# State-space scan at half the tokens, tiles in pairs, in the first layer of a three-block network

## Chip, cores, metric

One core of one Trainium2 chip. The metric is the device time of one execution in microseconds. Everything is fp32. The change touches one stage, the first mixing layer (class Fox in the code), which takes about the first 190 us of the kernel.

## The reference, cut to what matters

The network runs three blocks over 256 tokens of width 1024. The first block's mixer joins an attention with a forget gate (8 heads of 64) and a diagonal complex state-space scan over 32 groups of 16 channels with 64 states each:

```python
def s5_scan(u, a_re, a_im, log_dt, b_re, b_im, c_re, c_im, d_skip):
    dt = jnp.exp(log_dt)[:, None]
    mag = jnp.exp(a_re * dt)
    lb_re = mag * jnp.cos(a_im * dt)
    lb_im = mag * jnp.sin(a_im * dt)
    ...
    bu_re = jnp.einsum('bsgc,gpc->bsgp', u, bb_re)
    bu_im = jnp.einsum('bsgc,gpc->bsgp', u, bb_im)
    ...
    _, _, h_re, h_im = lax.associative_scan(combine, (a_re_t, a_im_t, bu_re, bu_im), axis=1)
    y = jnp.einsum('bsgp,gcp->bsgc', h_re, c_re) - jnp.einsum('bsgp,gcp->bsgc', h_im, c_im)
    return y + d_skip * u

def fox_s5_mixer(x, w_in, f_bias, ...):
    z = x @ w_in
    q, k, v, f_logit, u = jnp.split(z, ...)
    att = forgetting_attention(q, k, v, f_logit + f_bias)
    y = jax.nn.gelu(s5_scan(u, ...))
    y = y * jax.nn.sigmoid(y @ w_glu + b_glu)
    return jnp.concatenate([att, y], axis=-1) @ w_out
```

That is h(t) = L h(t-1) + B u(t), y(t) = Re(C h(t)), with a complex L per state.

## The kernel before, in words

All phases are written out by hand, one instruction stream per engine, with semaphores between them. Weights come through a ring of twelve 1 MB slots, filled by SyncE's DMA queue (L3019); a slot is filled again when the product that read it has ended. In this layer four slots are lent out as scratch memory, so eight are in use.

The scan works in tiles: 16 tiles j, each two groups (128 states on the partitions), with k = j // 4 and m = j % 4. A tile's two groups have 32 channels, which lie on partitions 32m to 32m+31 of `uT`. Instead of a complex recurrence the kernel turns the input by a phase table (cosine and sine of the angle of L times the token's place), scans with the real magnitude alone, and turns back:

- `tile_input` (L796): PE, two products of 32 rows by 256 tokens, real and imaginary part, into a bank.
- `turn_in` (L1143): VectorE, three operations on 512, 256 and 256 columns (L1155 to L1157).
- POOL adds the two halves (L1171), 512 columns.
- `scan` (L1161): VectorE, two scans over 256 tokens (L1166).
- `turn_back` (L1183): POOL, two products of 512 columns (L1193, L1194).
- `tile_output` (L805): PE, four products with 32 output columns each, side by side in the four 32-column groups of the array (L812 to L815); below, four such products are a quad.
- `keep_turn` (L828): ScalarE copies the four strips with signs.
- `tile_sums` (L818): PE, after every fourth tile, four products with a folding matrix, again side by side (L824).
- `y_keep` (L1135): VectorE, adds the skip term.

The order around it: `tensor` (L839) computes u (`first_product`, L925), the small strips for the forget gate (L281), tile inputs 0 and 1, the q and k projections (L268), then v in halves (L301) with tiles between them. Then comes the loop over tiles 3 to 15. Eight of its steps also carry an attention head: `scores` (L578: L588 and L790), `turn_p` (L593: L598) and `head_out` (L601: L606 and L608); on VectorE `head_max` (L624) and `head_scale` (L645), on ScalarE `head_exps`, `head_weigh`, `head_turned`, `head_kept` (L684 to L719). After the loop `mix_part` (L942: L946) starts the output product, then the gate (`fox_glu`) and the rest.

VectorE first prepares, from L1030 on: magnitude, sine and cosine, the output matrix times (L - 1)/a (`Cz`, 128x512), and the phase table for tokens 128 to 255 by seven doublings (`while n < P`, L1077). ScalarE mirrors it to the lower half (`mirror`, L1006). `Steps` (L67) makes each instruction of VectorE, ScalarE and POOL wait for the one before it on its engine.

Banks 0 and 1 hold the tile inputs, bank 2 sums, bank 3 outputs, banks 4 to 7 all else, each pair or set taken in turn.

Of the kernel before, what the change touches and what calls it, by code (L numbers as in the profile page):

```python
# [12 lines left out]
ACT = mybir.ActivationFunctionType  # L13
# [4 lines left out]
P = 128  # L18
SEQ = 256
# [329 lines left out]
class Start(Phase):  # L349
# [36 lines left out]
    def sync_second(self, sp):  # L386

        net, io, fox = self.net, self.net.io, self.net.phase_objects[1]
        for n, dst in enumerate(fox.C):
            sp.dma_start(dst, io["s5_c"][n].rearrange("p (k n) -> p k n", k=16)).then_inc(fox.s("params_loaded"), 16)  # L390
# [335 lines left out]
class Fox(Residual, Heads):  # L726
# [5 lines left out]
    HEAD_BEHIND = {5: 0, 6: 1, 8: 2, 9: 3, 10: 4, 12: 5, 13: 6, 14: 7}  # L732
# [4 lines left out]
    def __init__(self, net):  # L737
# [3 lines left out]
        self.uT = a.take(4 * SEQ, 4, SEQ)  # L741
# [4 lines left out]
        self.Cz = [a.take(512, 16, 32) for _ in range(2)]  # L746
        self.ut = a.take(1024)
        self.g = [self.ut[:, 0:512], self.ut[:, 512:1024], a.take(512)]
        self.t = a.take(512)
        self.w = a.take(20 * 16, 20, 16)  # L750
        self.ph = [a.take(16 * SEQ, 16, SEQ) for _ in range(2)]

        b = Arena(net.ring, self.LENT * UNIT)
        odd = [b.take(512) for _ in range(2)]
        self.C = [h.rearrange("p (a b) -> p a b", a=16) for h in odd]
        self.alloc_heads(b)
        self.sel = b.take(8 * P, 8, P, rows=8)
        self.ft = [b.take(SEQ, rows=8) for _ in range(6)]
        self.c_rows = b.take(16, NT, 8)
        self.strips = [b.take(SEQ) for _ in range(3)] + [a.take(SEQ)]  # L760
        self.f_strips = self.strips[0]
        self.turned = [[b.take(512) for _ in range(2)], odd]
        self.yT = self.catT[:, 4:8, :]
        self.mask = net.causal[:, :]
        self.sig = [self.B[0].rearrange("p a b -> p (a b)"), self.B[1].rearrange("p a b -> p (a b)")]

# [29 lines left out]
    def tile_input(self, pe, j):  # L796

        k, m = divmod(j, 4)
        t = self.net.T.open(pe, ("bu", j), self.INPUT)
# [3 lines left out]
        self.net.T.close(("bu", j), mm)  # L803

    def tile_output(self, pe, j):  # L805

        T = self.net.T
        t = T.open(pe, ("turn", j), self.TURN)
        pe.wait_ge(self.s("h_ready"), j + 1)
        by_cos, by_sin = self.turned[j % 2]  # L810
        re, im = slice(0, SEQ), slice(SEQ, 2 * SEQ)
        pe.matmul(t[0:32, re], self.Cz[0][:, j, :], by_cos[:, re], start=True, stop=True, skip_group_check=True)  # L812
        pe.matmul(t[32:64, re], self.Cz[1][:, j, :], by_cos[:, im], start=True, stop=True, skip_group_check=True)
        pe.matmul(t[64:96, re], self.Cz[1][:, j, :], by_sin[:, re], start=True, stop=True, skip_group_check=True)
        T.close(("turn", j), pe.matmul(t[96:128, re], self.Cz[0][:, j, :], by_sin[:, im], start=True, stop=True,  # L815
                                       skip_group_check=True))

    def tile_sums(self, pe, k):  # L818

        T = self.net.T  # L820
        t = T.open(pe, ("y", k), self.SUMS)
        pe.wait_ge(self.s("turn_kept"), 4 * k + 4)
        for m in range(4):
            mm = pe.matmul(t[32 * m:32 * m + 32, 0:SEQ], self.net.fold[:, 0:32], self.strips[m], start=True, stop=True,  # L824
                           skip_group_check=True)
        T.close(("y", k), mm)

    def keep_turn(self, act, j):  # L828

        net, T = self.net, self.net.T  # L830
        k, m = divmod(j, 4)
        if k:
            T.take(act, ("y", k - 1))
        t = T.take(act, ("turn", j))
        net.ac(act.activation(self.strips[m], t[:, 0:SEQ], ACT.Copy, scale=self.w[:, 19, 0:1]))
        T.free(act, ("turn", j))
        act.sem_inc(self.s("turn_kept"), 1)

    def tensor(self, pe):  # L839
# [5 lines left out]
        pe.wait_ge(self.s("params_loaded"), 16 * 4)  # L845
        pe.wait_ge(self.s("u_kept"), 4)
        for j in range(2):
            self.tile_input(pe, j)
# [4 lines left out]
        self.tile_input(pe, 2)  # L853
        vs = [net.use_unit(pe) for _ in range(2)]
        t = T.open(pe, ("fox_v", 0), rest)
        net.part(pe, t, vs, net.xT, 0, range(4))
        self.tile_input(pe, 3)
        self.tile_output(pe, 0)
        T.close(("fox_v", 0), net.part(pe, t, vs, net.xT, 0, range(4, KT)))
        self.tile_input(pe, 4)  # L860
        self.tile_output(pe, 1)
        t = T.open(pe, ("fox_v", 1), rest)
        net.part(pe, t, vs, net.xT, 1, range(4))
        self.tile_input(pe, 5)
        self.tile_output(pe, 2)
        T.close(("fox_v", 1), net.part(pe, t, vs, net.xT, 1, range(4, KT)))
        net.release([u for u, _ in vs], ("fox_v", 1))
        self.tile_input(pe, 6)
        pe.wait_ge(self.s("c_ready"), 1)
# [7 lines left out]
        for j in range(3, 16):  # L877
            self.tile_output(pe, j)
            if j == 3:
                self.scores(pe, 1)  # L880
# [2389 lines left out]
```

## Time and profile before

| | us |
|---|---|
| median of 3 runs | 1944.28 |
| lowest and highest | 1937.16, 1944.61 |
| profiled execution | 1941.67 |
| its span in the profile | 1939.5 |
| PE busy (share of the span) | 1799.3 (93%) |
| VectorE busy | 563.7 (29%) |
| ScalarE busy | 371.9 (19%) |
| POOL busy | 209.9 (11%) |

PE is TensorE's matmuls, PEld its weight loads, DVE VectorE, ACT ScalarE, POOL GpSimd, SP SyncE. A suffix q (POOLq) means the engine's sequencer. PEclk is the TensorE clock granted, as a share of 2.4 GHz. Every fp32 matmul shows as two records. Ends of matmuls are modelled and overlap the next start, so the distance between starts is the better measure of cost. "x8" counts records merged into a row; a bracket holds the idle time before it and what ended it.

### The profile page before, as it was taken

The page shows a single profiled execution, that of the slowest core. Times are in us where ns is not written, and L with a number is a line of the kernel's source. Part 1 is how long each engine was busy: PE and PEld are TensorE (multiplying, and loading weights), DVE is VectorE, ACT ScalarE, POOL GpSimd, SP SyncE. Part 2 cuts the span into 40 slices and gives each one's busy share as a digit, 9 for nine tenths or more (in the row PEclk, how much of TensorE's full clock was granted, in tenths as well). Part 3 has the DMA queues.
Part 4 walks back from the last instruction along what each step waited for, and adds up shares of the span by engine and source line. Part 5 has one row for each costly group of instructions (what it writes and reads, how often), then busy time and mean ns, then how long its engine had stood idle before and what let it go on. Part 6 is the DMA issues. An engine that isn't in the chain of part 4 may idle for free.

```text
span 1939.5 us, 21648 instructions
## 1 busy us (share of the span) xinstructions
PE 1799.3 (93%) x6956; PEld 934.2 (48%) x6957; DVE 563.7 (29%) x1236; ACT 371.9 (19%) x679; POOL 209.9 (11%) x403
## 2 busy tenths in 40 slices
PE   8998799899989989999989999999999988888886
PEld 6444333486633337855865475444443333232332
DVE  8882500587650031431372221011140000000002
ACT  1233311222221111032241100111032111110101
POOL 0561122000002310000000000000001110110100
PEclk9858899999989989999999999999999999999998
DMA  9002499676428993323413344332357999999995
GB/s 376 23 1 97 187 377 422 262 278 243 174 89 321 422 405 133 149 111 141 174 55 123 131 158 151 153 130 98 144 226 293 422 422 422 422 422 422 422 422 248
DMA packets 70439, 468.82 MB, mean 242 GB/s; under 512 B 7848, under 2 KB 12112, under 8 KB 15072
## 3 DMA queue, kind: packets, MB, share of 16 engines
q1 hardware_dynamic: 66016, 457.56, 58.1%
q10 hardware_dynamic: 4352, 10.35, 1.6%
q8 instruction: 40, 0.66, 0.1%
q14 instruction: 31, 0.25, 0.0%
HBM read 466.82 MB, written 1.06 MB: 241 GB/s over the span
## 4 chain that ended last, share of the span: by engine, by line
PE 67%; DMA 18%; DVE 10%; issue 2%; ACT 2%; SPq 0%; POOL 0%; DVEq 0%; ACTq 0%; POOLq 0%
PE bank L255 18%; DMA ring_sb<-stream 17%; PE bank L268 13%; PE bank L2705 10%; PE bank L1667 4%; PE bank L2748 4%; PE bank L2715 4%; PE bank L2642 2%; DVE scratch_sb L1027 2%; PE bank L301 2%; PE bank L946 1%; PE bank L1945 1%; DVE scratch_sb L1166 1%; DMA scratch_sb<-before 1%; PE bank L1302 1%
## 5 line engine op out<-in xcount | busy, mean ns | idle before, releaser
L2705 PE MATMUL bank<-ring_sb,scratch_sb 128*64 128x512 f32 x1536 | 347.3, 600 | 55.0 <-DMA ring_sb<-stream 48.8
L268 PE MATMUL bank<-xT_sb,ring_sb 128*128 128x256 f32 x1216 | 264.3, 379 | 0.0
L2705 PEld LDWEIGHTS bank<-ring_sb,scratch_sb 128*64 128x64 f32 x1536 | 115.4, 138 | 282.3 <-issue 273.2
L268 PEld LDWEIGHTS bank<-xT_sb,ring_sb 128*128 128x128 f32 x1216 | 230.6, 190 | 33.5 <-issue 2.5
L255 PE MATMUL bank<-ring_sb,xT_sb 128*128 128x512 f32 x416 | 179.4, 592 | 0.0
L255 PE MATMUL bank<-ring_sb,scratch_sb 128*128 128x512 f32 x384 | 167.7, 598 | 7.3 <-ACTq L2309 3.9
L2748 PE MATMUL bank<-ring_sb,scratch_sb 128*64 128x512 f32 x768 | 171.9, 596 | 0.0
L2866 DVE TENSOR_TENSOR scratch_sb<-scratch_sb,bank 128x256 f32<-128x256 f32 (+1 forms) x32 | 17.7, 554 | 408.9 <-PE bank L2705 278.7
L255 PEld LDWEIGHTS bank<-ring_sb,xT_sb 128*128 128x128 f32 x416 | 78.9, 190 | 97.7 <-issue 97.6
L2715 PE MATMUL bank<-scratch_sb 128*128 128x512 f32 x256 | 123.7, 606 | 0.0
L255 PEld LDWEIGHTS bank<-ring_sb,scratch_sb 128*128 128x128 f32 x384 | 73.1, 191 | 98.5 <-issue 90.6
L2982 ACT ACTIVATE scratch_sb<-bank 128x256 f32<-128x256 f32 (+1 forms) x96 | 47.1, 491 | 379.6 <-PE bank L2730 203.1
L2910 POOL COPY scratch_sb<-scratch_sb 128x256 f32 x128 | 45.2, 397 | 537.9 <-PEq L2608 525.7
L2871 DVE COPY scratch_sb<-bank 128x512 f32<-128x512 f32 x32 | 22.1, 692 | 277.7 <-PE bank L2748 277.7
L2748 PEld LDWEIGHTS bank<-ring_sb,scratch_sb 128*64 128x64 f32 x768 | 52.3, 137 | 96.8 <-issue 96.8
L1667 PE MATMUL bank<-ring_sb,xT_sb 128*128 128x512 f32 x192 | 84.5, 592 | 0.0
L2918 POOL TENSOR_SCALAR scratch_sb<-iota_sb,scratch_sb 128x64 f32<-128x64 f32 x128 | 71.7, 578 | 0.2
L2715 PEld LDWEIGHTS bank<-scratch_sb 128*128 128x128 f32 x256 | 43.5, 190 | 56.6 <-issue 56.6
L1667 PEld LDWEIGHTS bank<-ring_sb,xT_sb 128*128 128x128 f32 x192 | 36.3, 190 | 42.0 <-issue 41.6
L2985 ACT ACTIVATE scratch_sb<-bank 128x256 f32<-128x256 f32 (+1 forms) x32 | 15.7, 491 | 202.3 <-PE bank L2705 202.3
L2642 PE MATMUL bank<-scratch_sb 128*128 128x512 f32 x96 | 47.9, 663 | 6.8 <-DVEq L2813 6.8
L1361 DVE SCALAR_TENSOR_TENSOR scratch_sb<-ring_sb,mod_sb,scratch_sb 128x512 f32<-128x512 f32 x56 | 42.1, 752 | 2.9 <-DVE scratch_sb L667 0.2
(405 smaller groups left out, 1743.9 us busy)
## 6 DMA issues: line engine op xcount, KB each, us to landing
ring_sb<-stream SPq DMA_DIRECT2D x432, 1024.0 KB, 10.8
rows_sb<-rows ACTq DMA_DIRECT2D x12, 512.0 KB, 4.8
xT_sb<-xT SPq DMA_DIRECT2D x2, 512.0 KB, 7.1
x_sb<-x SPq DMA_DIRECT2D x1, 1024.0 KB, 19.9
scratch_sb<-bias_by_distance ACTq DMA_DIRECT2D x1, 1024.0 KB, 5.3
out<-x_sb ACTq DMA_DIRECT2D x2, 512.0 KB, 2.6
scratch_sb<-decay ACTq DMA_DIRECT2D x1, 768.0 KB, 5.4
small_sb<-small SPq DMA_DIRECT2D x1, 640.0 KB, 13.7
```

The source lines that it names most:

```text
L255: mm = pe.matmul(t[:, :], actT[:, k, i * P:(i + 1) * P], w[:, k % 4, :], start=k == 0, stop=k == kt - 1)
L268: mm = pe.matmul(t[:, m * SEQ:(m + 1) * SEQ], w[:, k % 4, n0:n0 + P], actT[:, k, :], start=k == 0, stop=k == kt - 1)
L301: mm = pe.matmul(bank[:, :], actT[:, k, i * P:(i + 1) * P], w[:, k % 4, :], start=k == 0, stop=k == kt - 1)
L1361: net.dv(dve.scalar_tensor_tensor(part, w[:, k, :], c, part, ALU.mult, ALU.add))
L1667: mm = pe.matmul(self.gate_bank[:, :], net.xT[:, kk, i * P:(i + 1) * P], w[:, k, :], start=kk == 0, stop=kk == KT - 1)
L2642: return pe.matmul(bank[:, :], self.src[:, i, k * P:(k + 1) * P], self.pick[i], start=i == 0, stop=i == 1)
L2705: mm = pe.matmul(t[e * TILE:(e + 1) * TILE, :], self.xs[e][:, kk, :], ws[e][:, k, :], start=kk == 0, stop=kk == KT - 1, skip_group_check=True)
L2715: pe.matmul(T.bank[2 * i + c][:, :], self.scatter[:, i * P:(i + 1) * P], self.y[:, c * 512:(c + 1) * 512], start=False, stop=False, skip_g ...
L2748: mm = pe.matmul(T.bank[6 + c][e * TILE:(e + 1) * TILE, :], self.hidT[:, ff, e * TILE:(e + 1) * TILE], ws[e][:, f, c * 512:(c + 1) * 512], ...
L2910: pool.tensor_copy(self.xs[e][:, 4 * m:4 * m + 4, :], self.xg[:, 4 * m:4 * m + 4, bass.ds(at[e] + tile * TILE, TILE)])\
L2918: pool.tensor_scalar(self.weigh[:, i, e * TILE:(e + 1) * TILE], self.net.iota[:, tile * TILE:(tile + 1) * TILE], self.of_pair[:, 0, i, e:e ...
L2982: act.activation(out, src, ACT.Copy).then_inc(self.tile_sem(f"freed{b}", over), 1)
```

## The change

The recurrence is run on every second token: the state at odd tokens is h(2n+1) = L² h(2n-1) + L B u(2n) + B u(2n+1). Odd outputs are read from it as before. Even outputs are y(2n) = Re(C L h(2n-1)) + Re(C B) u(2n): a lagged output matrix `E` and a direct term `K0`. Each scan then has 128 columns instead of 256, the phase table has 128 places per tile, and two tiles (of the same m, neighbouring k) form a pair p, so that an operation again covers 512 columns.

- Preparation: the output matrices are loaded compactly, 16 columns per tile instead of 32, plus a second compact copy of B; two DMAs more on SyncE's queue, the same bytes. VectorE computes L B, the output matrix and the lagged one in compact form and one doubling less of the table. ScalarE spreads four matrices (real and imaginary) into their block form, 16 activations on 64 partitions; POOL clears that memory. PE turns L B by products with the identity (`lag_weights`, 32 matmuls) and computes the direct weights (`direct_weights`, 32 matmuls).
- PE order: `lag_weights` stands right behind the small strips and waits for four spread matrices; pair inputs 0 and 1 and `direct_weights` stand between q and k; two scores more stand before and among the v products.
- ScalarE order: the copy of the direct weights stands before the forget gate's logarithm and the mirror; the first head's exponentials stand behind both copies of v.
- Loop: pairs 2 to 7. The sum after turning in moves from POOL to VectorE. Sums are taken after every pair, each fold behind the last in one column group, with the direct term added.
- `uT` is written with even and odd tokens apart, and `y_keep` reads them back in order.

The diff, cut to its core:

```diff
-    HEAD_BEHIND = {5: 0, 6: 1, 8: 2, 9: 3, 10: 4, 12: 5, 13: 6, 14: 7}
+    HEADS_BEHIND = ((), (0,), (1,), (2,), (3,), (4,), (5,), (6, 7))
...
+    def lag_weights(self, pe):
+        T = self.net.T
+        pe.wait_ge(self.s("spread"), 8)
         for part in range(2):
-            mm = pe.matmul(t[:, part * SEQ:(part + 1) * SEQ], self.B[part][32 * m:32 * m + 32, k, :],
-                           self.uT[32 * m:32 * m + 32, k, :], start=True, stop=True)
+            t = T.open(pe, ("lag", part), self.STATE)
+            for k in range(4):
+                for m in range(4):
+                    mm = pe.matmul(t[32 * m:32 * m + 32, k * P:(k + 1) * P], self.LBs[part][:, 4 * k + m, :],
+                                   self.net.ident[:, :], start=True, stop=True, skip_group_check=True)
+            T.close(("lag", part), mm)
+    def direct_weights(self, pe):
...
+        pe.wait_ge(self.s("spread"), 16)
+        for k in range(4):
+            for m in range(4):
+                j, out = 4 * k + m, t[32 * m:32 * m + 32, 32 * k:32 * k + 32]
+                pe.matmul(out, self.Bs[0][:, j, :], self.Cz[0][:, j, :], start=True, stop=False, skip_group_check=True)
+                mm = pe.matmul(out, self.Bs[1][:, j, :], self.Cz[1][:, j, :], start=False, stop=True,
+                               skip_group_check=True)
...
+    def pair_input(self, pe, p):
+        t = self.net.T.open(pe, ("bu", p), self.INPUT)
+        for odd in range(2):
+            k, m = self.tile(p, odd)
+            rows = slice(32 * m, 32 * m + 32)
+            for part in range(2):
+                at = (2 * odd + part) * self.HALF
+                out = t[:, at:at + self.HALF]
+                pe.matmul(out, self.LB[part][rows, k, :], self.uT[rows, k, 0, :], start=True, stop=False,
+                          skip_group_check=True)
+                mm = pe.matmul(out, self.B[part][rows, k, :], self.uT[rows, k, 1, :], start=False, stop=True,
+                               skip_group_check=True)
...
+            for even, weights in ((1, self.E), (0, self.Cz)):
+                at = odd * SEQ + (0 if even else n)
+                cols, of = slice(at, at + n), slice(0, n) if even else slice(1, n + 1)
+                for n4, (c, h) in enumerate(((0, by_cos[:, re, of]), (1, by_cos[:, im, of]), (1, by_sin[:, re, of]),
+                                             (0, by_sin[:, im, of]))):
+                    mm = pe.matmul(t[32 * n4:32 * n4 + 32, cols], weights[c][:, j, :], h, start=True, stop=True,
+                                   skip_group_check=True)
...
+    def pair_sums(self, pe, p):
...
+        for odd in range(2):
+            k, m = self.tile(p, odd)
+            rows = slice(32 * m, 32 * m + 32)
+            pe.matmul(t[rows, odd * SEQ:(odd + 1) * SEQ], self.net.fold[:, 0:32],
+                      self.strips[p % 2][:, odd * SEQ:(odd + 1) * SEQ], start=True, stop=False, skip_group_check=True)
+            mm = pe.matmul(t[rows, odd * SEQ:odd * SEQ + self.HALF], self.K0[rows, k, :], self.uT[rows, k, 0, :],
+                           start=False, stop=True, skip_group_check=True)
...
+        for p in range(2, 8):
+            self.pair_output(pe, p)
+            self.pair_sums(pe, p - 1)
+            if p + 2 < 8:
+                self.pair_input(pe, p + 2)
+            for h in self.HEADS_BEHIND[p]:
+                self.turn_p(pe, h - 1)
                 if h >= 2:
                     self.head_out(pe, h - 2)
                 if h + 2 < HEADS:
                     self.scores(pe, h + 2)
...
+        for p in range(8):
+            self.turn_in(dve, p)
+            self.scan(dve, p)
...
+        s(dve.tensor_tensor(self.g[p % 3], self.g[p % 3], self.t, ALU.add))
...
+        for odd in range(2):
+            for part in range(2):
+                at = (2 * odd + part) * n
+                xs = self.g[p % 3][:, at:at + n]
...
+                self.net.dv(dve.tensor_tensor_scan(xs, mag, xs, 0.0, ALU.mult, ALU.add))
```

## Rows read from the trace of the kernel before

**Rows 1.** Busy us (records) of PE, PEld, DVE, ACT, POOL; PEclk, DMA share, GB/s: the loop.
```profile
82.00:154.00 72.00, 65.59 (x265) 33.07 (x263) 59.89 (x98) 29.09 (x79) 42.72 (x34) 0.55 0.00 1
```
**Rows 2.** The same view for PE alone, ten us of the loop.
```profile
130.00:140.00 10.00, 10.00 (x35) 0.50 0.00 0
```
**Rows 3.** Timeline of DVE and POOL (start, us, what): a step with a head; the last scans.
```profile
92.68 0.69 DVE L1155 TENSOR_TENSOR scratch_sb<-bank,scratch_sb 128x512 f32<-128x512 f32 x1 [0.35 <-DVE scratch_sb L1138]
94.52 1.26 POOL L1171 TENSOR_TENSOR scratch_sb<-scratch_sb 128x512 f32<-128x512 f32 x1 [3.01 <-DVEq L1159]
94.53 2.53 DVE L1166 TENSOR_TENSOR_SCAN scratch_sb<-scratch_sb 128x256 f32<-128x256 f32 x2 [0.24 <-DVE scratch_sb L1157]
99.53 0.69 DVE L1155 TENSOR_TENSOR scratch_sb<-bank,scratch_sb 128x512 f32<-128x512 f32 x1 [0.25 <-DVE ring_sb L661]
...
151.79 1.65 DVE L1166 TENSOR_TENSOR_SCAN scratch_sb<-scratch_sb 128x256 f32<-128x256 f32 x2
```
**Rows 4.** Waits of SP's queue, 0 to 260 us: total, times, longest.
```profile
SPq L3019 <- PE bank L268: 152.9, 3, 125.2
```
**Rows 5.** Timeline of PE at full clock: scores, then transpose and head output, then output product.
```profile
82.87 0.48 PE L588 MATMUL bank<-scratch_sb 64*128 64x128 f32 x2
84.94 0.40 PE L812 MATMUL bank<-ring_sb,scratch_sb 128*32 128x256 f32 x1
159.29 0.55 PE L598 MATMUL bank<-ident_sb,ring_sb 128*128 128x128 f32 x3 [1.82 <-ACTq L704]
160.56 0.42 PE L824 MATMUL bank<-ring_sb,fold_sb 128*32 128x256 f32 x3
161.27 9.49 PE L946 MATMUL bank<-ring_sb,scratch_sb 128*128 128x512 f32 x18
```
**Rows 6.** Groups by form: us in total, mean ns; then idle time before.
```profile
L1027 DVE TENSOR_TENSOR scratch_sb<-scratch_sb 128x256 f32<-128x256 f32 x6 | 2.5, 425 | 0.2
L1027 DVE TENSOR_TENSOR scratch_sb<-scratch_sb 128x1024 f32<-128x1024 f32 x6 | 7.4, 1226 | 0.2
L703 ACT ACTIVATE ring_sb<-ring_sb 128x256 f32<-128x256 f32 x8 | 4.1, 507 | 0.3
```
**Rows 7.** Timeline of PE at half clock: transpose, head output, scores; input, output, sums.
```profile
113.62 0.90 PE L598 MATMUL bank<-ident_sb,ring_sb 128*128 128x128 f32 x3
115.93 0.79 PE L588 MATMUL bank<-scratch_sb 64*128 64x128 f32 x2
116.65 0.79 PE L790 MATMUL bank<-ring_sb 8*128 8x128 f32 x2
119.53 1.91 PE L801 MATMUL bank<-scratch_sb 32*128 32x256 f32 x4
138.21 2.07 PE L801 MATMUL bank<-scratch_sb 32*128 32x256 f32 x4
140.21 0.64 PE L812 MATMUL bank<-ring_sb,scratch_sb 128*32 128x256 f32 x1
141.06 0.65 PE L824 MATMUL bank<-ring_sb,fold_sb 128*32 128x256 f32 x3
```
**Rows 8.** Timeline of PE before the loop, at full clock but for 59.32.
```profile
26.16 1.14 PE L801 MATMUL bank<-scratch_sb 32*128 32x256 f32 x8
27.75 27.89 PE L268 MATMUL bank<-xT_sb,ring_sb 128*128 128x256 f32 x128
57.90 1.50 PE L801 MATMUL bank<-scratch_sb 32*128 32x256 f32 x4 [2.25 <-DVEq L111]
59.32 6.68 PE L301 MATMUL bank<-ring_sb,xT_sb 128*128 128x512 f32 x8
71.30 1.12 PE L801 MATMUL bank<-scratch_sb 32*128 32x256 f32 x4
72.36 0.40 PE L812 MATMUL bank<-ring_sb,scratch_sb 128*32 128x256 f32 x1
72.92 3.70 PE L301 MATMUL bank<-ring_sb,xT_sb 128*128 128x512 f32 x8
```

More of the change, by code:

```diff
@@ L740, in __init__ @@
         self.catT = a.take(8 * SEQ, 8, SEQ)
-        self.uT = a.take(4 * SEQ, 4, SEQ)
+        self.uT = a.take(4 * SEQ, 4, 2, SEQ // 2)
         self.qT = a.take(4 * SEQ, 4, SEQ)
@@ L837, in keep_turn @@
+    def keep_turn(self, act, p):
+        net, T = self.net, self.net.T
+        t = T.take(act, ("turn", p))
+        net.ac(act.activation(self.strips[p % 2], t[:, :], ACT.Copy, scale=self.w[:, 19, 0:1]))
+        T.free(act, ("turn", p))
         act.sem_inc(self.s("turn_kept"), 1)
@@ L844, in tensor @@
         net.small_strips(pe, "fox_f", "fox_f", net.xT, banks=self.STATE)
[L845 to L848, printed above, removed]
+        self.lag_weights(pe)
         pe.wait_ge(net.sem("strips_kept"), 1)
@@ L959, in scalar @@
         net.keep_strips(act, "fox_f", self.f_strips)
+        act.wait_ge(self.s("cleared"), 1)
+        act.wait_ge(self.s("prepared"), 1)
+        for part in range(2):
+            self.spread(act, self.LBs[part], self.compact(part, 1))
+        act.wait_ge(self.s("params_loaded"), 16 * 6)
+        for part in range(2):
+            self.spread(act, self.Bs[part], self.Bc[part])
+        for part in range(2):
+            t = T.take(act, ("lag", part))
+            s(act.activation(self.LB[part].rearrange("p a b -> p (a b)"), t[:, :], ACT.Copy))
+            T.free(act, ("lag", part))
+            act.sem_inc(self.s("u_kept"), 1)
+        act.wait_ge(self.s("prepared"), 2)
+        for n, dense in ((2, self.Cz), (3, self.E)):
+            for part in range(2):
+                self.spread(act, dense[part], self.compact(part, n))
+        self.keep_turns(act, "fox_q", self.qT, 0.125)
+        t = T.take(act, "direct")
+        s(act.activation(self.K0.rearrange("p a b -> p (a b)"), t[:, 0:P], ACT.Copy))
+        T.free(act, "direct")
         act.wait_ge(self.s("f_ready"), 1)
@@ L963, in scalar @@
         act.sem_inc(self.s("log_ready"), 1)
[L964 to L972 removed]
+        self.mirror(act)
+        self.keep_turns(act, "fox_k", self.kT, 1.0)
         for i in range(NT):
@@ new lines, in gpsimd, with turn_back @@
+        po(pool.memset(self.blocks, 0.0))
+        pool.sem_inc(self.s("cleared"), 1)
+        po(pool.memset(self.w[:, 19, :], 1.0))
+        po(pool.memset(self.w[96:128, 19, :], -1.0))
+        for pair in self.turned:
+            for v in pair:
+                po(pool.memset(v[:, :, 0:1], 0.0))
+        for p in range(8):
+            self.turn_back(pool, p)
+    def turn_back(self, pool, p):
+        net, T, n = self.net, self.net.T, self.HALF
+        cr, ci = (table[:, self.tiles(p), :].unsqueeze(2).to_broadcast([P, 2, 2, n]) for table in self.ph)
+        g = self.pair_of(self.g[p % 3])
+        u, t = (v[:, :, 1:n + 1].rearrange("p (o a) n -> p o a n", o=2) for v in self.turned[p % 2])
+        pool.wait_ge(self.s("g_ready"), p + 1)
+        if p >= 2:
+            T.take(pool, ("turn", p - 2))
+        net.po(pool.tensor_tensor(u, g, cr, ALU.mult))
+        net.po(pool.tensor_tensor(t, g, ci, ALU.mult))
```

371 lines of the change are left out of this document (182 added, 189 removed).

## Prediction, made before the changed kernel had run

> **What bounds the kernel now.** I read the stretch of the first layer (start to 161 us) by four views: busy time by stretch, the PE timeline at either clock level, the DVE and POOL timeline of one step, and what the weight queue waits for.
>
> The scan loop runs from about 82 to 154 us. In it PE is busy 65.59 of 72 us, at a mean granted clock of 0.55, and DVE 59.89 [rows 1]. So two engines bound it together: a DVE that got infinitely fast could give back at most PE's idle time, 72 - 65.6 = 6.4 us, as long as the clock stays where it is. And the clock does not stay low because PE rests: from 130 to 140 us PE is busy all ten microseconds and is granted 0.50 (1.2 GHz) [rows 2]. The reader is to see here that the engine with the low share (DVE) is the one the change relieves, and the one with no slack (PE) is the one it loads.
>
> On DVE a step of one tile with one head takes 92.68 to 99.53 = 6.85 us [rows 3]. Two scans of 256 columns take 1.65 us undisturbed (at 151.79), but 2.53 when they begin with POOL's sum (94.52, 1.26 long). Halving the columns and moving that sum to DVE removes both.
>
> The next 1 MB weight block is not what ends this stage: SP waits 125.2 us for a PE result in one piece [rows 4]. The stream stands still until PE is through, so what this stage gains or loses goes unchanged into the end of the kernel. PE begins the output product at 161.27 [rows 5]; my sum is the new time of that moment.
>
> **DVE after the change.** A pair costs 0.69 (128x512 from the bank [rows 3]) + 2 x 0.42 + 0.69 (the sum, now here) + 4 scans of 128 columns at half of 0.83 = 1.7, with gaps about 4.2 us; the 0.42 is the 128x256 form [rows 6]. A head adds what is left of the step: 99.53 - 94.53 - 2.53 = 2.5 us. Eight of each make 54 us where the 16 steps spread over some 97. The table loses its last doubling, 6 operations of 1.23 us [rows 6], and preparation gains 19 of 128x256 (8 us) for the 6 of 128x512 (4.4 us) it had, so the table is ready only about 2 to 4 us earlier. That is hidden: the ScalarE copy of the direct block now stands before the logarithm and the mirror, and it waits for PE. POOL's two products per pair (2 x 1.26) lie beside DVE's heads. All of this I cost at nothing, as long as PE needs more than 6.7 us per pair and head. If PE needed less, DVE would be next.
>
> **PE, piece by piece.** fp32 matmuls show as two records. At half clock [rows 7]: four records of 32x128 by 256 columns take 138.21 to 140.21, 0.50 each; streaming 256 columns takes 0.43 (a quad of four 32-column groups, two passes, 140.21 to 141.06). So 0.07 of a record is weight load that is not hidden. At full clock [rows 8]: 71.30 to 72.36, 0.265 each, of which 0.05 is exposed over 0.215; a quad takes 0.56 with the change of shape behind it.
> - Pair input: 16 records of 128 columns instead of 8 of 256. Half clock: 16 x (0.215 + 0.07) = 4.6 us against 4.0. Bounds: no load exposed, 3.4; every record at the 0.36 of the 64-row, 128-column kind (below), 5.8.
> - Pair output: 4 quads of 128 columns instead of 2 of 256. Half: 8 x 0.215 + 0.1 = 1.8 us (full 1.1). Bounds 1.7, and 3.4 if a narrow quad costs as much as a wide one; I stay near the streaming row, since the quads show next to no exposed load.
> - Pair sums: the old ones put four tiles side by side in column groups, 141.06 onwards, under 1 us per four tiles. A pair's two tiles lie in the same group, so two folds of 256 columns go one behind the other, 2 x 0.86, and two direct terms of 128 columns, 2 x (0.43 + 0.1): 2.8 us at half, 1.7 at full. Bounds 2.6 and 3.4.
> - Unchanged per head: transpose and head output 113.62 to 115.93 = 2.3, scores 115.93 to 119.53 = 3.6 [rows 7]; two records of the scores' 64-row, 128-column kind take 0.72. At full clock: scores 82.87 to 84.94 = 2.07, the other two 159.29 to 160.56 = 1.3 [rows 5].
>
> An iteration of pair and head is then 4.6 + 1.8 + 2.8 + 2.3 + 3.6 = 15.1 us at half clock and 2.5 + 1.1 + 1.7 + 1.3 + 2.1 = 8.6 at full. The old kernel needs for the same work at half clock 4.0 + 1.7 + 0.5 + 2.3 + 3.6 = 12.1. PE work per pair rises by a quarter.
>
> The input row also shows an exception: at 26.16 eight records of two tiles took 1.14 us, not 2.1 [rows 8], because they lie in different row groups. In the new order only pairs 0 and 1 stand together like this.
>
> The Trainium skill (TensorE: Matmul & The Clock Gate, section LDWEIGHTS (loading the stationary operand)) says that a load goes by its columns, so that 32x128 costs what 128x128 does, by its formula some 0.107 us; its section The mechanism adds that a load hides behind a running matmul only if the row group differs. That rule speaks against the narrow inputs; by it an input would be 16 x 0.32 = 5.1 us, an estimate, and the sum 2 us higher. The overlap at 26.16 agrees with the second part.
>
> **The sum for PE's clock time** (granted clock as in the rows).
> 1. Strips end as before at 26.2. New: PE waits for the four blocks that ScalarE spreads, with the transposes for head, projections and sums queued behind. ScalarE is free at about 26.7, when it has copied the strips (0.5); eight half-height copies at about 0.51 [rows 6] end at 31.0. +4.8 us. (The DVE product they need is done near 21.)
> 2. Lag weights: 32 matmuls, 8 quads of 128 columns, 0.43 each: 34.4. Small transposition 0.5: 34.9.
> 3. q projection: half of 27.89 [rows 8] = 13.9, 48.8. After an idle time of 2.25 us the first eight records of 512 columns took 6.68 instead of 3.70 [rows 8], at half clock; here the idle time is longer, so +3.0: 51.8.
> 4. Inputs 0 and 1, overlapping: 2.5, 54.3. Direct weights: 64 tiny records, no row is like them. Low end 1 us: an eighth of a quad's 0.43 pass, four side by side. High end 9 us: 64 times the 0.145 by which the scores' 64-row record (0.36) exceeds its streaming (0.215). I take 4, between them and nearer the quads, whose column groups they use: 58.3.
> 5. k projection 13.9, and one more fall of the clock, 3.0, since 6 us of small pieces precede it and 5 us follow: 75.2. In between, ScalarE's direct copy, logarithm and mirror run; scans start near 63.
> 6. To the loop, at full clock: input 2.5, three scores 6.2, four half products of v 14.8 (3.70 each), two outputs 2.2, input 2.5, sums 1.7, small transposition 0.3: 30.2, so 105.4.
> 7. Loop at half clock: p=2 without head output 13.6; p=3 to 5, 45.3; p=6 without input 10.5; p=7 with two heads 9.2; last transposition, output, sums 5.1: 83.7. The end is 189.1.
>
> Against 161.27 that is +27.8 us. The profiled execution took 1941.67 us (span 1939.5), so the sum is 1969.5; that execution lies 2.6 us under the median of the runs shown, 1944.28. The case's own bounds (inputs, outputs, sums, direct weights, the assumed fall of the clock) are about -13 and +24 us: 1956 to 1993.
>
> **Rivals.**
> - *PE at full clock throughout the loop.* For: DVE no longer makes PE wait, and the clock did rise in spots after dense pieces. The Trainium skill (the same page, section Why this matters for your kernels) advises an engine kept busy as the way to the full level. Against: a fully busy PE at 0.50 [rows 2]. Price: no fall in step 5 (-3), loop 48 + about 3 of waits for ScalarE at the end: 102.4 + 51 = 153.4, -7.9 us, 1934.
> - *Ends faster: DVE was the bound, and narrow pieces cost by columns alone.* Place: the loop's inputs, outputs and sums; price: at full clock 7.2 us an iteration instead of 8.6, and the front cheaper by 7; decides from the point at which no weight load is exposed and the clock stays up. 95.5 + 44 = 139.3, -22 us, 1920. Against it: the exposed 0.05 and 0.07 us per record [rows 7, 8].
> - *Clock half and half.* The loop at the mean of 83.7 and 48: 171.3, +10 us, 1952.
> - *The change doesn't act where it says*: the DVE sum, which now reads SBUF twice, waits for POOL as the scan did at 94.53. At most 2.5 us per pair, 6.7 + 2.5 = 9.2 us per pair: below 15.1, so it costs nothing at half clock.
>
> **How the numbers follow.** A measurement of this kernel tells about 0.5% (9.7 us) from no change. Forecast case 0.62, all slower. Full clock 0.14, about half of it within 0.5% and half just over. Cheap and full 0.08, faster. Half and half 0.16, split between slower 0.09 and same 0.07. So slower 0.71, same 0.14, faster 0.15. The likeliest time is 1969.5; its own range is 1956 to 1993. The range for 8 in 10 goes down to the full-clock case, 1936, and up to 1990; what is left out is cheap and full, part of the full-clock case and the top of the forecast's.
>
> **What the changed profile would show.** Right: PE idle about 5 us after the strips; granted clock near 0.5 between about 105 and 185 with PE busy over 95%; DVE busy near 60% there and waiting for PE or ScalarE; the output product beginning near 189; iterations of 15 us. Wrong: pair inputs under 3.5 us at half clock, a mean clock above 0.75 in the loop, or the output product beginning before 161.

## The result, and the profile after

| | before | after |
|---|---|---|
| median of 15 runs each, us | 1940.03 | 1949.81 |
| lowest and highest, us | 1935.17, 1946.29 | 1939.46, 1956.76 |
| profiled execution and span, us | 1941.67, 1939.5 | 1944.48, 1942.7 |
| VectorE, POOL busy, us | 563.7, 209.9 | 526.8, 170.9 |
| PE busy, us | 1799.3 | 1803.2 |

The ratio after to before is 1.0045, 95% interval 1.0028 to 1.0062: slower by 9 us, where I had forecast 28. The direction held, the size didn't: a third of it came.

The scan loop by stretch, with the columns of [rows 1]; the last two stretches are ten microseconds of it:

```profile
82.00:154.00 72.00, 69.47 (x464) 40.36 (x462) 31.19 (x74) 28.37 (x75) 12.66 (x10) 0.78 0.00 1
120.00:130.00 10.00, 10.00 (x35) 6.58 (x33) 6.60 (x15) 2.17 (x7) 0.00 (x0) 0.50 0.01 2
136.00:146.00 10.00, 10.00 (x83) 6.48 (x82) 5.64 (x13) 4.63 (x12) 2.54 (x2) 1.00 0.01 2
```

VectorE's busy time fell from 59.89 to 31.19 us and POOL's from 42.72 to 12.66, and PE's rose from 65.59 to 69.47. VectorE's relief came in full, 28.7 us; whether VectorE was the bound is asked below. But the mean granted clock, 0.55 in [rows 1], is 0.78 here. The window flatters the kernel after: up to 96 us it holds work that stands ahead of the loop there, all at full clock. From the loop's first output to the output product the two kernels have 0.56 and 0.70:

```profile
84.00:161.00 77.00, 68.72 (x284) 34.08 (x282) 58.06 (x96) 31.65 (x85) 43.51 (x34) 0.56 0.00 1
96.00:164.00 68.00, 63.23 (x407) 36.76 (x408) 31.40 (x75) 27.26 (x74) 12.66 (x10) 0.70 0.00 1
```

PE is fully busy in both of the ten-microsecond rows, once at 0.50 and once at 1.00. My sum had put the loop at 0.50 throughout.

Now PE's timeline ahead of the loop, the rows that answer to [rows 8] (start, duration, what, idle time in brackets):

```profile
30.23 3.51 PE L817 MATMUL bank<-ident_sb,scratch_sb 128*32 128x128 f32 x64 [4.61 <-ACTq L1079]
34.09 14.08 PE L268 MATMUL bank<-xT_sb,ring_sb 128*128 128x256 f32 x64
48.09 0.48 PE L852 MATMUL bank<-scratch_sb 32*128 32x128 f32 x2
51.52 0.28 PE L829 MATMUL bank<-scratch_sb 128*32 128x32 f32 x7
52.30 14.08 PE L268 MATMUL bank<-xT_sb,ring_sb 128*128 128x256 f32 x64
66.32 0.48 PE L852 MATMUL bank<-scratch_sb 32*128 32x128 f32 x2
```

The new wait of 4.61 us stands where it should, ahead of the lag product (L817). Both projections ran their 14.08 us at full clock. The same view in the loop: one iteration at the lower clock (117.00 to 131.58), one at the full clock that has no input (141.49 to 147.48), and the end.

```profile
117.00 1.94 PE L873 MATMUL bank<-scratch_sb 128*32 128x128 f32 x32
118.73 1.06 PE L886 MATMUL bank<-ring_sb,fold_sb 128*32 128x256 f32 x2
121.83 0.79 PE L852 MATMUL bank<-scratch_sb 32*128 32x128 f32 x2
125.54 0.90 PE L599 MATMUL bank<-ident_sb,ring_sb 128*128 128x128 f32 x3
131.58 1.94 PE L873 MATMUL bank<-ring_sb,scratch_sb 128*32 128x128 f32 x32
...
141.49 1.08 PE L873 MATMUL bank<-scratch_sb 128*32 128x128 f32 x32
142.39 0.60 PE L886 MATMUL bank<-ring_sb,fold_sb 128*32 128x256 f32 x2
144.13 0.55 PE L599 MATMUL bank<-ident_sb,ring_sb 128*128 128x128 f32 x3
147.48 1.08 PE L873 MATMUL bank<-ring_sb,scratch_sb 128*32 128x128 f32 x32
...
154.60 0.90 PE L599 MATMUL bank<-ident_sb,ring_sb 128*128 128x128 f32 x3 [3.12 <-ACTq L705]
158.62 0.90 PE L599 MATMUL bank<-ident_sb,ring_sb 128*128 128x128 f32 x3 [1.65 <-ACTq L705]
163.68 1.55 PE L1005 MATMUL bank<-ring_sb,scratch_sb 128*128 128x512 f32 x3
```

The output product begins at 163.68 against 161.27 [rows 5], +2.4 us of the spans' +3.2. It has two parts. From the start of the kernel to the loop's first output it is 96.51 (the loop begins with pair 2 there) against 84.94, +11.6. From there on it is 67.2 against 76.3 us, -9.2. The two parts don't hold the same work: of the +11.6, 4.1 are two scores of 2.07 us that stood in the loop before, and the front also has one more tile's input and output than before. New in it are the wait of 4.6 us and the lag product. The loop's part owes much to the clock: by the mean granted clock of the two rows above some 9 of 77 us are at the full level before, and 27 of 68 after.

The waits of PE in the stretch from 56 to 171 us (total, times, longest), first before, then after:

```profile
PE bank L812 <- POOLq L1195: 4.9, 3, 2.6
PE bank L598 <- ACTq L704: 3.3, 4, 1.8
PE bank L801 <- DVEq L111: 2.2, 1, 2.2
```
```profile
PE bank L599 <- ACTq L705: 4.8, 2, 3.1
```

The waits for VectorE and POOL are gone, 7.1 us of them; the one for ScalarE at the last heads is 1.5 us longer. As to the weight blocks: the longest wait of their queue for PE is 115.4 us where it was 125.2 [rows 4], so the stream still stands still until PE is through.

### The profile page after: what moved, and what is told of

Its sections match the earlier page's. It is cut to its first block, busy times and chain, and to the rows that moved or that the text cites. A ratio compares the mean times of both kernels' runs of the same rounds, so it can differ in the third digit from the quotient of the medians.

```text
span 1942.7 us, 22232 instructions
## 1 busy us (share of the span) xinstructions
PE 1803.2 (93%) x7308; PEld 947.7 (49%) x7309; DVE 526.8 (27%) x1226; ACT 376.0 (19%) x690; POOL 170.9 (9%) x376
## 4 chain that ended last, share of the span: by engine, by line
PE 73%; DMA 17%; DVE 5%; ACT 2%; issue 2%; SPq 0%; POOL 0%; ACTq 0%; DVEq 0%; POOLq 0%
PE bank L255 18%; DMA ring_sb<-stream 17%; PE bank L268 14%; PE bank L2816 10%; PE bank L1778 4%; PE bank L2859 4%; PE bank L2826 4%; PE bank L2753 2%; PE bank L301 2%; PE bank L2056 1%; PE bank L1005 1%; PE bank L589 1%; PE bank L995 1%; PE bank L1413 1%; PE bank L607 1%
## 6 DMA issues: line engine op xcount, KB each, us to landing
ring_sb<-stream SPq DMA_DIRECT2D x432, 1024.0 KB, 11.6
```

## The experiments

All ratios are to the kernel before, run beside each kernel on the same chip; the kernel after has 1.0045. "Lower clock" is worked out from each run's mean granted clock c as 2(1 - c) x span, the time at 1.2 GHz, and is a median over the runs (a step in the clock's last digit is 4 us). The kernel before itself differed from chip to chip: 1937.6 us with 139 us at the lower clock beside a2, a3, a4 and b1; 1943.3 with 151 beside a1, d1, d2 and d3; 1937.4 with 136 beside e1, e3, e4 and g1; 1940.0 with 140 beside h1, h2 and h3. So kernels are compared by their ratios, and the last column only roughly where the chips differ.

| kernel | median us | ratio, 95% interval | lower clock, us |
|---|---|---|---|
| before (80 runs of it) | about 1940 | 1 | 139 |
| after | 1949.81 | 1.0045 (1.0028 to 1.0062) | 129 |
| a1_before_half_scan | 1935.58 | 0.9970 (0.9955 to 0.9985) | 135 |
| a2_lag_late | 1947.14 | 1.0043 (1.0017 to 1.0069) | 136 |
| a4_dve_load | 1952.13 | 1.0068 (1.0049 to 1.0088) | 142 |
| a3_sums_by_four | 1933.87 | 0.9977 (0.9960 to 0.9995) | 112 |
| b1_both | 1934.17 | 0.9978 (0.9961 to 0.9994) | 120 |
| d1_inputs_beside | 1922.56 | 0.9912 (0.9891 to 0.9933) | 88 |
| e1_two_in_turn | 1943.53 | 1.0027 (1.0015 to 1.0038) | 128 |
| h2_beside_front | 1938.82 | 0.9993 (0.9980 to 1.0006) | 120 |
| h3_beside_loop | 1932.39 | 0.9953 (0.9934 to 0.9971) | 100 |
| h1_beside_dve_load | 1939.90 | 0.9990 (0.9976 to 1.0004) | 122 |
| g1_before_beside | 1949.00 | 1.0050 (1.0032 to 1.0067) | 154 |
| d2_beside_and_sums | 1925.20 | 0.9916 (0.9900 to 0.9933) | 104 |
| d3_all_three | 1927.05 | 0.9923 (0.9906 to 0.9941) | 112 |
| e3_inputs_later | 1928.19 | 0.9948 (0.9932 to 0.9964) | 119 |
| e4_lag_own_wait | 1922.44 | 0.9919 (0.9904 to 0.9935) | 88 |

**Was VectorE the bound?** Two kernels ask, from both sides. The first is the kernel before with each scan over half of its columns:

```diff
-            xs = self.g[j % 3][:, part * SEQ:(part + 1) * SEQ]
+            xs = self.g[j % 3][:, part * SEQ:part * SEQ + P]
...
```

> The kernel before, with each scan made over the first 128 of its 256 tokens only (the scan of the other 128 tokens is left out), so that VectorE loses about half of its scan work, 32 pieces of 128 elements or some 20 us, and TensorE's work is as it was. It is VectorE's relief of the change, alone. If TensorE is the bound, little comes of it: the POOL waits of the kernel before ahead of its outputs (0.6, 1.7 and 2.6 us) shrink, 0 to 6 us less than before, about 1936 us. If VectorE's chain bounds the kernel before, 20 us or more go: 1920 us.

0.9970, 6 us less (the interval says 3 to 9), at the end of what the PE theory allowed. But this run can't part the two theories, since far less than 20 us left VectorE. Its scans in the trace, before and in a1:

```profile
L1166 DVE TENSOR_TENSOR_SCAN scratch_sb<-scratch_sb 128x256 f32<-128x256 f32 x32 | 40.9, 1278 | 4.7 <-DVE scratch_sb L1157 4.0
L1166 DVE TENSOR_TENSOR_SCAN scratch_sb<-scratch_sb 128x128 f32<-128x128 f32 x32 | 32.5, 1016 | 4.7 <-DVE scratch_sb L1157 4.0
```

That is 8.4 us, less than a third of the relief of the change: POOL's sum still runs beside the scans. A gain of 3 to 9 us fits a bound VectorE as well as waits that shrink. The waits speak for the second: the output product begins at 157.96, 3.3 us earlier, and the three POOL waits of 4.9 us are two of 0.7 and 2.0, so 2.2 us went there. The lower clock fell too, from 151 us beside it to 135. That PE bounds the kernel before rests on its busy rows; no run shows it. The second loads VectorE in the kernel after:

```diff
-        s(dve.tensor_tensor(self.pair_of(self.g[p % 3]), b, cr, ALU.mult))
+        for _ in range(4):
+            s(dve.tensor_tensor(self.pair_of(self.g[p % 3]), b, cr, ALU.mult))
```

> The kernel after, with VectorE's first multiply of each pair's scan input made four times instead of once: 3 x 0.425 us x 2 or about 2.2 us more VectorE work for each of the 8 pairs, 18 us in all (the result is the same). If TensorE sets the end of this stretch and VectorE has slack (idle blocks of 15.6, 6.2 and 4.5 us in the loop of the kernel after), the time rises by 0 to 4 us. If VectorE is the bound, it rises by about 18 us, to 1968 us.

1.0068 against 1.0045: 4 us by the ratios, and the intervals overlap. Of 17 us more work on VectorE a quarter is seen; the intervals leave room for some 9 us, not for 17. From 56 to 171 us PE waits 0.7 us for POOL and 3.1 for ScalarE in this trace, no more than in the kernel after. VectorE is not the bound of the kernel after.

**The wait in the front.** The lag product moved behind the q product:

```diff
-        self.lag_weights(pe)
         pe.wait_ge(net.sem("strips_kept"), 1)
         ...
         net.product_T(pe, "fox_q", net.xT, banks=rest)
+        self.lag_weights(pe)
```

> The kernel after, with the lag weights made behind the q product instead of ahead of it; nothing else is changed. TensorE waited 4.61 us for ScalarE ahead of L817 at 30.23 us of the kernel after, and the q product needs nothing of it. If TensorE's own sequence sets the end, the wait goes and the 3.5 us of the lag product stay: about 4.5 us less than the kernel after, some 1945 us. If the front's wait is only the first of several that the loop would make good later (VectorE or ScalarE is the bound there), the time stays at about 1950 us and the idle time reappears ahead of the inputs or of the first output.

1.0043: no gain can be seen, though the intervals are too wide to rule out the 4.5 us of the first theory. The trace shows how it could be. Timeline of PE in this kernel:

```profile
26.54 14.08 PE L268 MATMUL bank<-xT_sb,ring_sb 128*128 128x256 f32 x64
40.55 1.95 PE L817 MATMUL bank<-ident_sb,scratch_sb 128*32 128x128 f32 x64
43.43 0.45 PE L852 MATMUL bank<-scratch_sb 32*128 32x128 f32 x2 [0.93 <-ACTq L1030]
48.41 16.44 PE L268 MATMUL bank<-xT_sb,ring_sb 128*128 128x256 f32 x64
64.78 0.48 PE L852 MATMUL bank<-scratch_sb 32*128 32x128 f32 x2
```

q begins 7.5 us earlier, k ends 1.5 us earlier. The kernel after had the lower clock directly behind its wait, from 30 to 33 us, where it made the lag product 3.51 us long instead of 1.95. Here the clock stayed up there and fell behind the small products at 46 us instead, until 52, and k took 16.44 us. The rest went into a wait of 0.93 us for the copy of the lag weights and into the small products at the lower clock.

**The sums.** Once for four pairs, four groups of columns side by side:

```diff
+        if p % 4 != 3:
+            return
 ...
-            pe.matmul(t[rows, odd * SEQ:(odd + 1) * SEQ], self.net.fold[:, 0:32],
-                      self.strips[p % 2][:, odd * SEQ:(odd + 1) * SEQ], ...)
+            for m in range(4):
+                pe.matmul(t[32 * m:32 * m + 32, odd * SEQ:(odd + 1) * SEQ], self.net.fold[:, 0:32],
+                          self.strips[m][:, odd * SEQ:(odd + 1) * SEQ], ...)
```

> The kernel after, with the closing sums over the states and the direct products made once for four pairs, the four row tiles one behind the other in four groups of columns, instead of once for each pair in one group of columns. If TensorE is the bound and its small products run side by side only in different groups of columns, eight times 1.76 us (3.1 us at the lower clock) become two times some 2 to 3 us: 8 to 15 us less than the kernel after, 1935 to 1942 us. If the sums are hidden (TensorE waits for VectorE or ScalarE in the loop anyway), nothing comes of it, 1950 us. If products in different groups of columns do not overlap at all, the busy time of these rows is the same and the time stays too: then the row of four pairs is 7 us at full clock.

0.9977: 13 us less than the kernel after by the ratios, and just faster than before. In its trace, mostly at the lower clock (0.67 from 117 to 120 us), eight folds and eight direct products side by side:

```profile
117.20 1.92 PE L889 MATMUL bank<-ring_sb,fold_sb 128*32 128x256 f32 x16
119.05 0.64 PE L894 MATMUL bank<-scratch_sb 32*32 32x128 f32 x16
119.62 0.48 PE L854 MATMUL bank<-scratch_sb 32*128 32x128 f32 x2
```

That is 2.4 us for four pairs, where one pair's sums took 3.1 at the lower clock (118.73 to 121.83 above) and 1.7 at the full. The third row shows the shape of the pair input, back at full clock. The sums were on PE's path: made pair by pair, in one group of columns, they cost more than the whole loss of the change. Together with the moved lag product:

> The lag weights behind the q product and the sums by four pairs together. If both act on the same sequence of TensorE, their gains add: 12 to 20 us less than the kernel after, 1930 to 1938 us, at or below the kernel before. If the loop is bound by another engine once TensorE has less, the two together give no more than the larger of them alone.

0.9978, no less than the sums alone. No worth of the move is seen here either; the gains don't add.

**The pair inputs.** Both tiles of a pair lie in the same group of 32 rows. Two neighbouring pairs don't. Their inputs made together, in two banks, product by product in turn (at 0, at 2, and in the loop at 4 and 6):

```diff
+        ts = [self.net.T.open(pe, ("bu", q), self.INPUT) for q in (p, p + 1)]
+        for odd in range(2):
+            for part in range(2):
+                at = (2 * odd + part) * self.HALF
+                for n, w in ((0, self.LB), (1, self.B)):
+                    for q, t in zip((p, p + 1), ts):
+                        ...
+                        mm = pe.matmul(t[:, at:at + self.HALF], w[part][rows, k, :], self.uT[rows, k, n, :], ...)
```

> The kernel after, with the inputs of two neighbouring pairs made together, product by product in turn, so that each product is in another group of rows and another bank than the one ahead of it (four times, instead of eight inputs alone). If TensorE is the bound and products of different groups of rows run side by side, each two inputs take some 2 us instead of 3.8 at full clock and 4 instead of 7.4 at the lower: 7 to 11 us less than the kernel after, 1939 to 1943 us. If the narrow products are held up by something that they share (the load of their weights), the rows stay at 3.8 us and the time with them. If the earlier inputs make TensorE wait for a bank that VectorE still reads, an idle time of 1 to 3 us stands ahead of them and takes part of the gain.

0.9912: 26 us less than the kernel after and 17 less than before, more than any theory had. The same products in the same places, but one pair behind the other, tell whether it was the place:

> The kernel with the inputs of two pairs together, its products in the same place of TensorE's order, but all of the first pair and then all of the second, so that nearly all neighbours share their group of rows. The kernel with them side by side stood 27 us under the kernel after; its rows (3.4 to 3.8 us for two inputs become about 2) explain some 6 to 8 us of that, and the rest came with 88 us at the lower clock where the kernel after has 129. Theory: both come of the products running side by side; then this kernel loses both again and stands at 1943 to 1950 us with 115 us or more at the lower clock. Rival: the gain comes of the place (inputs two at a time, no input ahead of output 0); then it stands at 1925 to 1930 us with the clock of the kernel with them side by side.

1.0027. By the ratios the place gives 3 us (the intervals overlap), the products side by side 22. e4 below, which is d1 with a shorter wait, ran beside e1 on the same chip: 1922.4 against 1943.5 us, with 88 against 128 us at the lower clock. The same two inputs in the front, first in turn, then side by side:

```profile
47.56 3.49 PE L853 MATMUL bank<-scratch_sb 32*128 32x128 f32 x32
```
```profile
48.31 2.05 PE L853 MATMUL bank<-scratch_sb 32*128 32x128 f32 x32
...
97.29 2.05 PE L853 MATMUL bank<-scratch_sb 32*128 32x128 f32 x32
110.48 2.05 PE L853 MATMUL bank<-scratch_sb 32*128 32x128 f32 x32
```

Four times 1.4 us are 6 of the 22. The rest is the clock: 128 us at the lower level became 88, and 40 us at half the rate hold 20 us of work at the full. The loop of this kernel, from behind its first input to the last heads, with the columns of [rows 1]:

```profile
99.00:136.00 37.00, 33.03 (x319) 19.36 (x316) 25.98 (x63) 21.61 (x58) 11.42 (x9) 1.00 0.00 1
```

It stays at 1.00 for all of 37 us. Where is that won? Side by side in the front only, or in the loop only:

> Inputs side by side for pairs 0 to 3 only, those of pairs 4 to 7 in the same place but one pair behind the other. The rows give back 2 x 1.75 us at full clock, 2 x 3.4 us at the lower. If only the rows count, 1926 to 1929 us. If what stands in the loop sets its clock, some 30 us more of it are at the lower clock and the time is 1936 to 1944 us.

> The other way round: side by side for pairs 4 to 7 only, those of pairs 0 to 3 one behind the other, at full clock, so 3.5 us more in the rows. If only rows and the loop's clock count, 1926 to 1929 us. If the inputs of the front set the clock of what follows, it is 1936 us or more.

0.9993 and 0.9953. Against the ones in turn the front gives 7 us, the loop 14, together the 21 to 22 of both. So each place has its own rows (2.9 us) and its own share of the clock (8 and 28 us less at the lower level, worth up to 4 and 14). The first is as its second case said, the rows and part of the clock; the other lies between its two cases.

**Does the relief of VectorE pay then?** The load on VectorE of a4, now with the inputs side by side:

> Inputs side by side, with VectorE's first multiply of each pair made four times: 17 us more VectorE work, as on the kernel after, where it cost about 3 us. If TensorE is the bound here too, 0 to 5 us more than 1922.6 us. If VectorE's relief is what lets the inputs side by side pay (the kernel before, with its full scans, lost 10 us by them, with TensorE waiting for POOL up to 5.5 us ahead of its outputs), the load costs 12 us or more: 1935 us and above, with such waits in its trace.

0.9990, 15 us more than without it by the ratios (the intervals leave 10 to 20), where the same load cost 4 in the kernel after. But not by the waits that I expected. PE's waits in this trace, 56 to 171 us:

```profile
PE bank L599 <- ACTq L705: 4.8, 2, 3.1
PE bank L853 <- DVEq L111: 2.4, 2, 1.4
```

The two waits for VectorE's banks are 2.4 us together. Behind the second, which ends at 99.57, the loop by stretch shows this:

```profile
99.00:137.00 38.00, 37.43 (x223) 22.61 (x223) 29.25 (x63) 10.91 (x29) 10.12 (x8) 0.51 0.00 1
```

Nearly the stretch that stood at 1.00 without the load is at 0.51, with PE busy 37.43 of its 38 us. At the lower clock are 122 us in all instead of 88, worth 17. The waits cost little, what followed them much. That the wait brought the lower clock is the likely reading of one trace, not shown. The other side is the kernel before with its inputs side by side, two tiles at a time from tile 2 on:

```diff
+            if j % 2 and j + 3 < 16:
+                self.tile_inputs(pe, j + 3)
```

> The kernel before, with the inputs of two neighbouring tiles made together, part by part in turn, from input 2 on (0 and 1 were so already). Seven times 4.1 us at the lower clock become some 2.2 us. If TensorE is the bound in the kernel before too and the lower clock goes back with the denser products, 10 to 25 us less than before: 1915 to 1930 us, and the decimation is worth nothing beside it. If VectorE and POOL then bound it (16 tiles of full length, against 8 pairs of half), TensorE waits for them ahead of the outputs, and the gain is 8 us at most: 1932 us or above.

1.0050, slower by 10 us: the second case's side and mechanism, but with a loss where it had a small gain. Its waits:

```profile
PE bank L814 <- POOLq L1193: 18.7, 8, 5.5
PE bank L598 <- ACTq L704: 3.8, 4, 1.8
PE bank L802 <- DVEq L111: 3.4, 1, 3.4
```

PE waits for POOL, the end of the chain VectorE, POOL, 18.7 us in eight places where it waited 4.9 in three. VectorE in turn waits for the inputs, every second of which comes a step later in this order; in the kernel before this wait is 0.2 us:

```profile
DVE scratch_sb L1153 <- PE bank L802: 10.1, 3, 5.6
```

So part of the loss can be that of late inputs, and that 16 full-length tiles leave VectorE too little room is argued, not shown. In the kernel after such an order gains 26 us, in the kernel before it loses 10. I tried no other placement of the inputs in the kernel before, so that none helps there is not shown.

**Further.** Four kernels on top of d1:

> Inputs of two pairs beside each other and the sums by four pairs together, on the kernel after. The sums by four gave 16 us against the kernel after. If the inputs act on the same sequence, 7 to 11 us more go: 1923 to 1928 us, faster than the kernel before by some 0.6%. If another engine bounds the loop by then (waits of TensorE for POOL were already 2.4 and 1.5 us where the sums go by four), the time stays near 1933 us and these waits grow by what the inputs gave.

> The same with the lag weights behind the q product as well. Moving them gave nothing that the runs could tell, although the q product then began 7.5 us earlier: the k product ended only 1.5 us earlier, 2.4 us of it by the lower clock. If that is how it always goes, this kernel stands at the time of the one without the move. If the move is worth something once the loop has less for TensorE to do, it is 2 to 5 us less.

> Inputs side by side and sums by four, with the inputs of pairs 4 to 7 behind the heads' products of their place instead of ahead of them. With both edits TensorE waited 2.65 us for VectorE's bank at 93 us, and the clock fell there for 12 us; the inputs side by side alone had neither. If that wait brought the lower clock, this kernel has 90 us or less of it and stands at 1914 to 1920 us. If the clock falls there anyway, it is 1922 to 1926 us. If the inputs now come too late, TensorE waits for POOL ahead of outputs 4 and 6, 2 us or more each, and the time is 1925 us or above.

> Inputs side by side, and the lag product waits for the spread of its own four blocks only, not for that of the four blocks behind them, which only the direct product reads. ScalarE takes some 2 us for these four, so that TensorE's wait of 4.6 us ahead of it falls to some 2.5 us. If the front's wait counts in full, 2 us less than 1922.6 us; if the lower clock that follows it takes them back, as with the lag weights moved, no difference.

None gained: d2 and d3 stand where d1 does, e3 is some 7 us behind. With the sums by four PE has less to do, and waits appear in the loop: 2.65 us for a bank of VectorE's at 93 us in d2; with the inputs later (e3) 3.0 for ScalarE, then 1.2 and 2.8 for POOL. The lower clock rose from 88 us to 104 in d2, 112 in d3 and 119 in e3. e3's expectation took the wait at 93 for the cause of the lower clock; with that wait gone another came, so it does not tell. e4 began the lag product 1.7 us earlier (wait 2.65 instead of 4.62) and no gain is seen, as with a2; 2 us would be inside the intervals. d1, d2, e4 and d3, 0.9912 to 0.9923, can't be told apart, and all four are faster than both kernels of this study.

## Why the prediction was wrong, step by step

The step that failed is step 7, the level of the clock in the loop: 83.7 us forecast, 67.2 measured. Behind it come the terms ahead of the loop, above all the two falls of the clock (steps 3 and 5) and the direct weights (step 4).

- **What bounds the kernel: right for the kernel after,** where of a load of 17 us on VectorE 4 were seen and PE's sums gave 13. For the kernel before it isn't shown: 8.4 us less work on VectorE gave 3 to 9 us. The most that I had left a faster VectorE was PE's idle time, 6.4 us.
- **Step 1, wait for the spread, +4.8: right,** 4.61. Its worth is another matter: a2 and e4 took it away or cut it and gained nothing measured.
- **Step 2, lag and small transposition: right,** from 30.23 to 34.09, 3.9 us for 3.9. Its 0.43 us a quad is the price at the lower clock, which the step didn't say, and the clock was low there (0.57 from 30 to 34 us); at full clock the lag product took 1.95 us (a2).
- **Step 3, fall of the clock in q, +3.0: failed.** The lower clock came with the wait and the lag product and was over when q began.
- **Step 4, inputs 0 and 1 overlap, 2.5 us: failed, 3.4.** All of pair 0 stands ahead of pair 1, and neighbours share their rows; interleaved it is 2.05 (d1). **Direct weights, 4 us: failed, 0.8** (51.52 to 52.30), under even the low end. The 64 tiny records, four groups of columns side by side, took 0.05 us for each four; my high end came from the scores' 64-row products, which aren't split by columns.
- **Step 5, fall in k, +3.0: failed,** 14.08. In a2 it came (16.44), so the step was possible, not certain.
- **Step 6, to the loop, 30.2: right,** 52.30 + 14.02 to 96.51 is 30.2; that 1.7 us of it are v at the lower clock (5.40 instead of 3.70) hides that the small pieces were priced a little high.
- **Step 7, loop at half clock, 83.7: failed, and it is the largest term.** 67.2 us. Its iteration was sized well: 14.58 at the lower clock for 15.1, 6.0 at the full for 8.6 - 2.5 = 6.1 (the terms of the 8.6 add up to 8.7). Wrong was that every iteration would be at the lower one; 41 us of the loop in the profiled run were. "Clock half and half", given 0.16, has 65.9 us for the loop and was the rival that came there; its front was as much too long as the forecast's. (In the rival "Ends faster" 95.5 + 44 is 139.5, not 139.3.)
- **Pair input: 4.6 was too much.** 121.83 to 125.54, 3.7 us, near the bound without exposed load (3.4); at full clock 136.16 to 138.14, 2.0 for 2.5. I had taken 0.07 us of load per record from the wide rows. The Trainium skill (TensorE: Matmul & The Clock Gate, section LDWEIGHTS (loading the stationary operand)) would have made it 5.1, an estimate that adds a load priced by its columns to every record. The loads do go by columns in the trace (0.20 us for one of 32x128, 0.19 for one of 128x128, means from 48 to 165 us), but they weren't added: a record took 0.23 us at the lower clock for 0.215 of streaming. By its section The mechanism a load overlaps a running matmul only where the row group differs; here they were nearly hidden in one row group too, so the trace doesn't agree. What two row groups gave is more than hidden loads: 32 records side by side took 2.05 us instead of 3.49, less than their 3.4 us of streaming at full clock, so the products themselves ran side by side.
- **The sum in SBUF waits for POOL:** seen once, 1.47 us for 0.69 when POOL's products ran beside it, and costless, as said.

The steps ahead of the loop were 8.9 us too long, the loop 16.5, together 25.4, against the 25.0 by which the profiled execution (1944.48) missed 1969.5. One step of reasoning is behind most of it: from "PE fully busy at 0.50" [rows 2] I concluded that the loop's level is 0.50 for this work. The row only said that being busy is no cure. The runs of one kernel spread by 17 us with the clock as they do: 1938.1 us of span at 0.973, 1951.0 at 0.963, 1955.0 at 0.961 in the kernel after. I had put the level into rivals only, and my forecast's own range, 1956 to 1993, held none of it.

What stays open is what exactly sends the clock down. It did so behind waits (4.6 us at the lag product, 3.1 at the last heads, 1.4 in h1) and also behind small products with no wait (at 71 and at 101 us in the kernel after, at 93 in d1). No run here separates the two causes.

## What to carry to other kernels

Relief on an engine that isn't the bound can pay through another edit: 17 us of load put back on VectorE cost 4 us in the kernel after, and 15 once the products of PE stood side by side. So try the two together, with the load put back as a control, and read from the trace how much work a control really moved: half of the scans' columns was 8.4 us, not 20. When small products replace large ones, place neighbours in different groups of rows or columns (and different banks), and when a kernel's time follows its granted clock, forecast the share of time at each level as a term with its own bounds.

## What the runs showed that I had not expected

- Products of the same work side by side instead of in turn: 6 us in the rows, 22 in the time. 40 us less at the lower clock.
- 1.4 us of waiting were followed by 36 us at the lower clock (h1).
- 32 products (64 records) of 128 rows by 32 columns, in four groups of columns, took 0.8 us.
- Removing a wait of 4.6 us of the bounding engine gave no time that 8 runs can show.
- Loads of 32x128 weights were nearly hidden behind products of the same row group: 16 records in 3.71 us at the lower clock, 3.4 of it streaming.
